# Splitting token rows in plain order: a mixture-of-experts gather whose stationary operand is read with a stride of eight elements

## The reference

```python
def grouped_moe(h, router_w, router_bias, w_gate, w_up, w_down):
    ...
    scores = jax.nn.sigmoid((xt @ router_w).astype(jnp.float32))
    ...
    out = jnp.zeros_like(xt)
    for e in range(N_EXPERTS):
        he = jax.nn.silu(xt @ w_gate[e]) * (xt @ w_up[e])
        out = out + (he @ w_down[e]) * gate[:, e:e + 1]
    return out.reshape(B, S, D)
```

## Time and profile before

| what | value |
|---|---|
| median of the runs shown | 848.75 us |
| the profiled execution | 844.93 us |
| its span | 843.1 us |
| mean granted clock of PE | 0.958 |
| busy: PE, DVE, ACT, POOL | 93%, 30%, 21%, 10% |
| read from HBM | 243.35 MB, 290 GB/s over the span |
| layer 0: first gather, experts | about 214 to 219 us, 220 to 440 us |
| layer 1: first gather, experts | about 607 to 612 us, 612 to 832 us |

### The profile page before, as it was taken

One profiled execution on the slowest core, in us unless ns is written; L12 is line 12 of the kernel. 1 busy time (PEld: TensorE's weight loads), 2 busy tenths in 40 slices (PEclk: granted clock), 3 DMA queues, 4 the chain that ended last, 5 costly groups with the idle time before them and its releaser, 6 DMA issues.

```text
span 843.1 us, 9010 instructions
## 1 busy us (share of the span) xinstructions
PE 782.8 (93%) x3761; PEld 410.9 (49%) x3761; DVE 255.7 (30%) x493; ACT 180.1 (21%) x429; POOL 87.3 (10%) x92
## 2 busy tenths in 40 slices
PE   6999999897999999999987999999799999999994
PEld 5877865544534333433335887544533443344331
DVE  3585165315111101110026774513510111101014
ACT  3444355303110001000003455611210100010000
POOL 0012134302000000000000220410300000000000
PEclk9999589998899999999997999999699999999998
DMA  9999300124199999999999755014259999999971
GB/s 303 366 397 403 131 1 2 51 100 149 68 431 428 429 426 428 427 428 428 427 390 387 290 199 181 21 51 144 106 230 430 428 428 428 428 427 428 426 335 51
DMA packets 38924, 245.03 MB, mean 291 GB/s; under 512 B 5344, under 2 KB 9568, under 8 KB 26592
## 3 DMA queue, kind: packets, MB, share of 16 engines
q1 hardware_dynamic: 38880, 244.41, 71.7%
HBM read 243.35 MB, written 1.05 MB: 290 GB/s over the span
## 4 chain that ended last, share of the span: by engine, by line
PE 85%; DVE 8%; ACT 3%; issue 2%; DMA 1%; DVEq 0%; SPq 0%
PE ps L590 26%; PE ps L608 13%; PE ps L619 7%; PE ps L561 7%; PE ps L433 4%; PE ps L434 4%; PE ps L435 4%; PE ps L582 4%; PE ps L468 2%; ACT R L914 2%; PE ps L482 1%; PE ps L568 1%; PE ps L416 1%; DVE small L1094 1%; DVE X L1158 1%
## 5 line engine op out<-in xcount | busy, mean ns | idle before, releaser
L590 PE MATMUL ps<-ring,R 128*64 128x512 f32 x1024 | 223.6, 594 | 7.3 <-ACT R L805 5.4
L590 PEld LDWEIGHTS ps<-ring,R 128*64 128x64 f32 x1024 | 73.0, 137 | 147.7 <-issue 139.8
L608 PE MATMUL ps<-ring,R 128*64 128x512 f32 x512 | 113.4, 595 | 3.1 <-DVE R L1215 3.1
L1212 DVE TENSOR_TENSOR R<-R,ps 128x512 f32<-128x512 f32 x16 | 17.2, 1072 | 237.9 <-PE ps L590 237.9
L1044 DVE TENSOR_TENSOR wl<-ring,wh 128x512 fp32r<-128x512 f32 x88 | 66.5, 770 | 48.7 <-ACT wh L789 48.5
L433 PE MATMUL ps<-wh,xh 128*128 128x512 f32 x176 | 72.1, 410 | 4.9 <-DVE wl L1044 4.8
L434 PE MATMUL ps<-wl,xh 128*128 128x512 f32 x176 | 70.6, 401 | 0.0
L435 PE MATMUL ps<-wh,xl 128*128 128x512 f32 x176 | 70.5, 400 | 0.0
L608 PEld LDWEIGHTS ps<-ring,R 128*64 128x64 f32 x512 | 35.3, 137 | 69.6 <-issue 64.0
L789 ACT CAST wh<-ring 128x512 fp32r<-128x512 f32 x88 | 54.2, 621 | 58.6 <-PE ps L435 58.6
L619 PE MATMUL ps<-R 128*128 128x512 f32 x128 | 59.2, 605 | 0.0
(11 more groups left out here) (149 smaller groups left out, 799.5 us busy)
## 6 DMA issues: line engine op xcount, KB each, us to landing
ring<-in_w_gate SPq DMA_DIRECT2D x32, 2048.0 KB, 17.1
ring<-in_w_up SPq DMA_DIRECT2D x32, 2048.0 KB, 17.8
ring<-in_w_down SPq DMA_DIRECT2D x32, 2048.0 KB, 20.8
ring<-in_w_in SPq DMA_DIRECT2D x22, 1024.0 KB, 14.0
ring<-in_w_out SPq DMA_DIRECT2D x8, 1024.0 KB, 15.0
ring<-in_cmp_kw SPq DMA_DIRECT2D x2, 1024.0 KB, 16.3
ring<-in_cmp_vw SPq DMA_DIRECT2D x2, 1024.0 KB, 13.4
R<-in_ln_g SPq DMA_DIRECT2D x4, 512.0 KB, 3.9
```

What stands on the lines that cost most here:

```text
L590: last = mm(ps[64 * e:64 * e + 64, to, :], xe[:, j, at + 64 * e:at + 64 * e + 64], slots[e][:, j * UNIT:(j + 1) * UNIT], start=(j == 0), s ...
L608: last = mm(ps[64 * e:64 * e + 64, 2 + w, :], hT[:, k, 64 * e:64 * e + 64], slots[e][:, at:at + UNIT], start=(k == 0), stop=(k == FJ - 1))
L1212: tt(hid.rearrange("p (k c) -> p k c", k=FJ), by_row(sg), by_row(ps[:, 1, :]), ALU.mult).then_inc(rd.h, 1)
```

## The change

The rounded tokens and their rests are stored in the order of X: both writers (ACT's cast and POOL's subtraction) now read and write contiguous rows of 1024 elements, and the gather picks chunk `j` itself, as every eighth element from `j` on, 32 bytes apart. No instruction, wait or DMA is added or removed, and the values that go into each product are the same.

```diff
-        Xp = [v[:, :, :].rearrange("p j t -> p (j t)").rearrange("p (a j c) -> p a j c", a=T, j=KJ) for v in (xh, xl)]
+        Xp = [v[:, :, :].rearrange("p j t -> p (j t)").rearrange("p (a n) -> p a n", a=T) for v in (xh, xl)]
...
-                            last = mm(ps[:, bank, at * n:(at + 1) * n], Xp[k][:, a, j, :],
+                            last = mm(ps[:, bank, at * n:(at + 1) * n], Xp[k][:, a, j::KJ],
                                       Pm[:, a].rearrange("p e c -> p (e c)")[:, 0:n],
                                       start=(a == 0 and k == 0), stop=(a == T - 1 and k == 1))
...
                 def rows_hi(a):
                     act.wait_ge(N.x_ready, ready(2 * l, a, 1))
-                    copy(Xp[0][:, a], X[:, a].rearrange("p (c j) -> p j c", j=KJ)).then_inc(R.xp, 1)
+                    copy(Xp[0][:, a], X[:, a]).then_inc(R.xp, 1)
...
                             pool.wait_ge(R.xp, C.xp + a + 1)
-                            tt(Xp[1][:, a], X[:, a].rearrange("p (c j) -> p j c", j=KJ), Xp[0][:, a], ALU.subtract
+                            tt(Xp[1][:, a], X[:, a], Xp[0][:, a], ALU.subtract
                                ).then_inc(R.xl, 1)
```

## The result

The changed kernel takes 875.2 us in the median of four runs (871.04 to 878.5), the kernel before in the same comparison 849.48 us. The ratio is 1.0295, with a 95% interval of 1.0258 to 1.0332: 25.7 us slower, where the forecast was 24.8 us over the median known then. The profiled execution took 878.5 us (span 876.7 us), the longest of the four.

A forecast was written before the change was run, and what follows sets the result against it. PE was taken to bound the expert stages, with the weight stream close behind. Gather 27.7 us, less 1.9 for waits and 0.9 for POOL, made 24.9 us more: 873.5 us forecast, range 851 to 885 us.

The forecast's parts named there:

- What bounds it: Expert stages: PE bounds them, the weight stream close behind; a longer gather lengthens the kernel equally, except for two waits.
- The price of the load: Gather (L582): a load of 128 columns 32 bytes apart takes 232 ns, 115 ns more per record.
- the rival in which the load scales with the clock: First gather groups: clock stays at 0.50, 15 us more for two layers, 888 us; chance 0.08, shared with prices over 138 ns.
- second witness: DVE's L1212, 16 bytes between elements, against L1204: 1.79 ns per element, taken to support ACT's 1.81 ns.
- The count: Gather records: 2.8 us per first group and 11.0 us for the other groups, 13.8 us per layer, 27.7 for two.
- Given back: Last pair of each layer: slower PE lets the weight stream get ahead, so waits of 1.28 and 0.61 us go, 1.9 us.
- POOL and the norm: First L999 of a layer, beside L1158: 2.39 us instead of 2.84, gaining 0.45 us per layer, 0.9 us in all.
- The cast: ACT's L926: 1.05 us in plain order, 1.0 us less, none of it on the path.
- The sum: Whole kernel: 27.7 - 1.9 - 0.9 = 24.9 us more, forecast 873.5 us, 2.9% slower.
- its first rival: Gather load has room and the norm gets shorter: 844 to 848 us, perhaps 1.6 us per layer from L574; chance 0.14.

The follow-up runs named there:

- A wait in another order: Against the kernel before: one more POOL wait, so a layer's first subtraction starts only when the second tile's X is ready; 844.45 us, ratio 0.9947.
- together with the shorter subtraction: Against the kernel before: chunks stored alternating in pairs, weight load at a stride of 2, plus the later first subtraction on POOL; 842.39 us, ratio 0.9924.
- the writers alone: Against the changed kernel: gather's weight load back in plain order, writers still contiguous, so unwanted columns are gathered; 848.52 us, ratio 0.9979.
- stride 2: Against the kernel before: split rows stored with chunks 2m and 2m+1 alternating by element, weight load at a stride of 2; 848.26 us, ratio 0.9966.

## Why the prediction was right

- **What bounds it.** PE was the chain in the expert stages, and a longer gather made the kernel longer by as much. Nothing covered it, as forecast.
- **The price of the load.** 115 ns per record were forecast from ACT's cast, 1.81 ns for each strided element. The runs show 125 ns in the groups of 8 (242 against 117), 1.88 ns per column. The reading of it as the time of a fetch, which doesn't go with the engine's clock, was right for PE too: 240 ns at a clock of 0.50 and at 1.00. That also ended the rival in which the load scales with the clock, worth 15 us. Its second witness was weaker than it was taken for: L1212 reads one of its two strided operands from PSUM, so its 1.79 ns may not be the price of the same thing.
- **The count.** 2.8 us per first group: 3.0 measured. 11.0 us for the twelve groups of a layer: 0.99 us more for each is 11.9. Together 27.7 forecast, 29.8 measured.
- **Given back.** Both waits of 1.28 and 0.61 us are gone.
- **POOL and the norm.** L999 was forecast at 2.39 us and has 2.35; 0.49 us of the norm went in layer 0. The ratio in the Trainium skill (GPSIMD Engine Reference, Performance pitfalls for Q7 kernels) would have had 1.9 us; the two-operand row L980 was the better guide. That was partly luck. The prediction took the fastest of 16 without a reason; the 512-element ones, 1672 ns in the median, would have given 2.9 ns per element and 3.2 us, no gain at all. The timeline has the reason: 13 of the 16 start 0.16 us behind DVE's L1044, which reads two SBUF operands, and take 1.12 us (256 elements) or 1.67 us (512). The three that have no such step beside them take 0.74 and 1.27 us, 2.1 ns per element. In layer 1 the clock had already fallen at L416 (1.98 us in the chain), and the gain is not to be seen there. The cast was forecast at 1.05 us and has 1.047.
- **The sum.** By the measured terms 29.8 - 1.9 - 0.5 = 27.4 us, with 24.9 forecast and 25.7 between the medians. The median came out 1.7 us above the forecast. Of that 0.7 us is the kernel before, whose median in the comparison is 849.48 us and not 848.75; the rest is on the side of the term that was too small: 10 ns more per record are 2.4 us over both layers.
- **What the forecast missed.** It held the norm's gain to be POOL's half microsecond, and had the clock behind it only in its first rival (1.6 us per layer). A wait in another order did more than the shorter instruction: 1.9 us of PE's idle time and 1.3 to 1.6 us under L574 in a layer, of which the routing's first step took 1.2 to 1.4 us back. Between the medians that was 4.4 us, and 6.4 us together with the shorter subtraction. None of this is in the time of the change itself.

## What to carry to other kernels

Before a stationary operand is given a stride, ask what paces the stream of loads and products: with 256 moving columns the load had no slack, and it paid 1.8 to 1.9 ns for every 16-byte line it opened. ACT's cast paid the same (1.81 ns at one element per line, 0.91 at two); POOL's subtraction lost only half a nanosecond per strided element (2844 against 2346 ns for 1024). A stride of two elements of 4 bytes costs next to nothing and made both sides cheap here, so a layout may be shared between writer and reader at two neighbours per line. And when a small elementwise step on POOL seems hidden, look at which DVE step with two SBUF operands stands beside it, and order POOL's work around that one.

## What the runs showed that was not expected

- A DVE instruction with two SBUF operands stood still until POOL's subtraction ended, however small it was: L1158 took 2.76 us instead of 0.74, and the routing's first step, 32 elements, 1.61 us instead of 0.24, each ending within 0.6 us of POOL's end, and the small one within 0.05 us. It goes the other way too: POOL's L980, two SBUF operands, took 1.12 us instead of 0.74 when it started behind DVE's L1044. DVE's steps that read PSUM were not slowed: L1148 took 0.7 us beside L999, and L1026 (L1027 in the later kernel) 0.69 us beside the two late subtractions.
- PE's idle time of 1.4 to 1.9 us ahead of L416 was followed each time by a granted clock of 0.50 under most or all of L574, 3.0 to 3.6 us; with none the 16 records took 2.0 to 2.6 us. This part of the gain was nearly as large as the one that was aimed at. Idle time is not the whole of it: with 0.5 to 0.6 us of it, and the clock already down before L416, L574 of layer 1 took 3.60 us in the changed kernel and 1.96 us with the writers alone and with stride 2. What decides there no run shows.
- 2 KB pieces instead of 16 KB in two thirds of the loads cost the stream 5 to 9% of its rate (391 to 406 GB/s against 428), and since it had run at 29.4 us per pair beside a PE at 27.7, nearly all of that became time.
- Granted clocks of stretches that no edit touches differ from run to run (0.82 and 0.86 in the attention of layer 0, 3 us). Single spans of this kernel should be compared by stage.
